# GpSimd adds at three borders, sums of squares in mid second gate and up, and ones by ones on TensorE at borders

## The reference, cut to what matters

```
# first stack
x = x + mix(rms_norm(x, g))
x = x + swiglu(rms_norm(x, g), w_gate_up, w_down)
# second stack
m = hybrid_rglru_mla(h) if layer % 2 == 0 else gated_delta_net(h)
x = x + rms_norm_2(m, norm_mix_post[layer])
h = rms_norm_2(x, norm_ffn_pre[layer])
x = x + rms_norm_2(swiglu_2(h, ...), norm_ffn_post[layer])
```

## Time and profile before

| | us |
|---|---|
| Runs shown: median (lowest, highest) of 3 | 2483.07 (2482.04, 2484.55) |
| The profiled execution: its own time | 2482.38 |
| The profiled execution: span of the page | 2480.6 |
| PE busy, DVE busy, ACT busy, POOL busy | 2309.6, 1563.7, 1186.7, 780.3 |

### The profile page before, as it was taken

How to read it: one execution, slowest core, us unless ns; L and a number is a source line. 1 busy time by engine, 2 the same in 40 slices (tenths; PEclk the granted TensorE clock), 3 DMA queues, 4 the chain that set the end, 5 groups by cost and what they waited for, 6 DMA issues and landing times.

```text
span 2480.6 us, 52063 instructions
## 1 busy us (share of the span) xinstructions
PE 2309.6 (93%) x20530; PEld 2218.5 (89%) x20530; DVE 1563.7 (63%) x2768; ACT 1186.7 (48%) x1956; POOL 780.3 (31%) x682
## 2 busy tenths in 40 slices
PE   7899787999999998899999999899997899999998
PEld 6899776999978988899999999789997898988997
DVE  3779787566631776666566666847667665536665
ACT  4544654544444665544444356544444445534333
POOL 1211588100068554300000037750003565554000
PEclk9999888999999999999999999999998999988999
DMA  4575200455536453455345554335552222223552
GB/s 172 202 200 179 95 1 1 136 195 183 173 125 193 142 140 114 137 186 177 128 162 183 181 164 147 123 99 188 184 186 75 74 78 88 76 86 118 181 192 85
DMA packets 103604, 344.30 MB, mean 139 GB/s; under 512 B 16400, under 2 KB 22064, under 8 KB 102912
## 3 DMA queue, kind: packets, MB, share of 16 engines
q1 hardware_dynamic: 102560, 339.61, 42.2%
q0 software_dynamic: 864, 2.16, 0.4%
HBM read 340.56 MB, written 1.16 MB: 138 GB/s over the span
## 4 chain that ended last, share of the span: by engine, by line
PE 69%; DVE 8%; ACT 4%; issue 2%; SPq 0%; POOL 0%; DMA 0%; DVEq 0%; ACTq 0%; POOLq 0%
PE ps L164 20%; PE ps L165 19%; PE ps L166 19%; ACT hi L102 1%; PE ps L289 1%; PE ps L1571 1%; DVE dr_aq L3338 1%; PE ps L3025 1%; DVE h_low L328 1%; PE ps L2976 1%; PE ps L1581 1%; DVE reciprocal_root L356 0%; PE ps L3018 0%; DVE lo L124 0%; PE ps L1594 0%
## 5 line engine op out<-in xcount | busy, mean ns | idle before, releaser
L164 PE MATMUL ps<-h_high,hi 128*128 128x256 f32 x3384 | 994.5, 294 | 47.1 <-DVE h_low L328 28.5
L165 PE MATMUL ps<-h_low,hi 128*128 128x256 f32 x3384 | 970.6, 287 | 0.0
L166 PE MATMUL ps<-h_high,lo 128*128 128x256 f32 x3384 | 970.2, 287 | 0.0
L102 ACT ACTIVATE hi<-raw 128x1024 fp32r<-128x1024 f32 x623 | 647.8, 1052 | 372.7 <-PE ps L166 371.8
L164 PEld LDWEIGHTS ps<-h_high,hi 128*128 128x128 f32 x3384 | 662.4, 196 | 65.6 <-DVE h_low L328 33.5
L165 PEld LDWEIGHTS ps<-h_low,hi 128*128 128x128 f32 x3384 | 663.2, 196 | 0.7
L166 PEld LDWEIGHTS ps<-h_high,lo 128*128 128x128 f32 x3384 | 662.3, 196 | 0.0
L124 DVE TENSOR_TENSOR lo<-raw,hi 128x1024 fp32r<-128x1024 f32 x422 | 509.7, 1224 | 214.4 <-ACT hi L102 213.9
L141 POOL TENSOR_TENSOR lo<-raw,hi 128x512 fp32r<-128x512 f32 x384 | 495.5, 1316 | 284.0 <-ACT hi L102 283.4
L164 PE MATMUL ps<-hidden_high,hi 128*128 128x256 f32 x1088 | 307.0, 282 | 5.0 <-DVE lo L124 3.3
L165 PE MATMUL ps<-hidden_low,hi 128*128 128x256 f32 x1088 | 308.6, 284 | 0.0
(11 more groups left out here) (470 smaller groups left out, 3278.2 us busy)
## 6 DMA issues: line engine op xcount, KB each, us to landing
raw<-in_weights SPq DMA_DIRECT2D x623, 512.0 KB, 3.5
at_bias<-bias_group SPq DMA_DIRECT2D x64, 64.0 KB, 2.8
consts<-in_consts SPq DMA_DIRECT2D x1, 1506.5 KB, 8.4
x<-in_x SPq DMA_DIRECT2D x1, 1024.0 KB, 4.8
s_cT<-in_s_b SPq DMA_DIRECT2D x1, 1024.0 KB, 7.5
s_cw<-in_s_c SPq DMA_DIRECT2D x1, 1024.0 KB, 9.5
s_parts<-in_s_bn SPq DMA_DIRECT2D x4, 256.0 KB, 9.3
s_cT<-s_rows POOLq DMA_DIRECT2D x16, 64.0 KB, 9.6
```

The costliest lines, as they stand in the source:

```text
L102: act.activation(k.hi[:, item % CUT, :], k.raw[:, item % RAW, :], ACT.Copy).then_inc(k.item_rounded, 1)
L164: pe.matmul(out, wh, xh, start=start, stop=False, **more)
L165: pe.matmul(out, wh, xl, start=False, stop=False, **more)
L166: return pe.matmul(out, wl, xh, start=False, stop=stop, **more)
```

## The change

Four things change, and one semaphore is shared to make room for a new one (`turned` replaces two).

- At the `POST` borders POOL does some of the adds of normed tiles to `x`: tiles 1 to 4 in the two feed-forwards, tiles 1 to 7 in the gated delta net. DVE keeps the others. POOL does them ahead of its adds of squares, or ahead of its weight cuts.
- In the two feed-forwards behind them, PE's sums of the new `x` move from before the second gate and up to its middle, between gate and up.
- PE multiplies ones by ones (128 x 128 by 128 x 128 in 32-bit floats, into PSUM bank 7) a number of times, ahead of the first gate and up: 20 at each of the three `POST` borders (after the sums of the result), 16 and 10 in the feed-forwards of layers 0 and 1, 8 in `glu`.
- The waits for `x` follow who writes the tile.

```diff
+def idle_products(k, pe, n):
+    for _ in range(n):
+        pe.matmul(k.ps[:, 7, 0:P], k.ones[:, :], k.ones[:, :], start=True, stop=True)
...
-    def __init__(self, k, gain_col, pending=0, post_col=None, cuts=True, adds=False):
+    def __init__(self, k, gain_col, pending=0, post_col=None, cuts=True, adds=False, idle=0):
+        self.idle = idle
+        self.pool_adds = () if pending != self.POST else range(1, KT - 3 if adds else KT)
+        self.b_px = k.x_added.n
+        k.x_added.n += len(self.pool_adds)
...
     def sums_before(self, pe):
         if self.pending == self.POST:
             self.sums(pe, 0)
+        idle_products(self.k, pe, self.idle)
...
     def gpsimd(self, pool):
-        for j in range(1, KT - 1):
+        for j in self.pool_adds:
+            pool.wait_ge(k.post_done.s, self.b_y + j + 1)
+            pool.tensor_tensor(k.x[:, j, :], k.x[:, j, :], k.post[:, j % 2, :], ALU.add).then_inc(k.x_added.s, 1)
+        for j in range(1, KT - 1) if self.adds else ():
...
     def vector(self, dve):
             if j < KT and self.pending == self.POST:
-                dve.wait_ge(k.post_done.s, self.b_y + j + 1)
-                dve.tensor_tensor(k.x[:, j, :], k.x[:, j, :], k.post[:, j % 2, :], ALU.add).then_inc(k.x_done.s, 1)
+                if j not in self.pool_adds:
+                    dve.wait_ge(k.post_done.s, self.b_y + j + 1)
+                    dve.tensor_tensor(k.x[:, j, :], k.x[:, j, :], k.post[:, j % 2, :], ALU.add).then_inc(k.x_done.s, 1)
...
             if j + 2 < KT and self.pending == self.POST:
-                dve.wait_ge(k.x_done.s, self.b_x + j + 1)
+                self.x_wait(dve, j)
                 normed(j + 2)
...
             def gate_up(i, b):
                 for half in range(2):
+                    if half == 1 and b == 1 and isinstance(i, int) and prep.pool_adds:
+                        prep.sums_after(pe)
...
             prep.x_read(pe)
-            prep.sums_after(pe)
+            if not prep.pool_adds:
+                prep.sums_after(pe)
...
 def glu(k, src, sg, pr, parts):
             w = Weights(k, pe, first)
+            idle_products(k, pe, 8)
...
-    swiglu(k, k.hp, Prep(k, VEC_AT["norm_ffn_pre_2"] + KT * layer, Prep.POST, VEC_AT["norm_mix_post_2"] + KT * layer, adds=True))
+    swiglu(k, k.hp, Prep(k, VEC_AT["norm_ffn_pre_2"] + KT * layer, Prep.POST, VEC_AT["norm_mix_post_2"] + KT * layer, adds=True, idle=20))
...
-    prep = Prep(k, VEC_AT["norm_mix_pre_2"] + KT, Prep.POST, VEC_AT["norm_ffn_post_2"], cuts=False)
+    prep = Prep(k, VEC_AT["norm_mix_pre_2"] + KT, Prep.POST, VEC_AT["norm_ffn_post_2"], cuts=False, idle=20)
...
+        prep.gpsimd(pool)
         late_cut(k, pool, late)
         cut(0, 8)
...
-    swiglu(k, k.hp, Prep(k, VEC_AT["norm_ffn_g"] + KT * layer, adds=True), side)
+    swiglu(k, k.hp, Prep(k, VEC_AT["norm_ffn_g"] + KT * layer, adds=True, idle=(16, 10, 0, 0)[layer]), side)
```

More of the change, by code:

```diff
@@ L252, in __init__ @@
         if pending:
-            k.x_done.n += KT
+            k.x_done.n += KT - len(self.pool_adds)
         if pending == self.POST:
@@ L272, in scalar @@
             if self.pending:
-                act.wait_ge(k.x_done.s, self.b_x + j + 1)
+                self.x_wait(act, j)
             else:
@@ L316, in here, with x_wait @@
         pe.wait_ge(self.k.low_done.s, self.b_l + j + 1)
+    def x_wait(self, engine, j):
+        if j in self.pool_adds:
+            engine.wait_ge(self.k.x_added.s, self.b_px + self.pool_adds.index(j) + 1)
+        else:
+            engine.wait_ge(self.k.x_done.s, self.b_x + sum(i not in self.pool_adds for i in range(j + 1)))
     def x_read(self, pe):
         if self.pending:
-            pe.wait_ge(self.k.x_done.s, self.b_x + KT)
+            pe.wait_ge(self.k.x_done.s, self.b_x + KT - len(self.pool_adds))
+            if self.pool_adds:
+                pe.wait_ge(self.k.x_added.s, self.b_px + len(self.pool_adds))
     def vector(self, dve):
@@ L820, in __init__ @@
         self.V, self.A, self.side, self.rows = k.s5v, k.s5a, k.side_here, k.s5_rows
-        self.flipped, self.masked = k.s5_flipped, k.s5_masked
+        self.flipped, self.masked = k.turned, k.s5_masked
         self.v, self.a0, self.s0 = k.s5v.n, k.s5a.n, k.side_here.n
@@ L927, in done @@
         self.k.s5a.n += 6
+        self.flipped.n += 1
         self.k.s5v.n = self.v
@@ L2724, in gdn_heads @@
     g.x = k.sem("gdn_x_updated")
-    g.xt = k.sem("gdn_x_turned")
     g.u = k.sem("gdn_u_in_psum")
@@ L2737, in gdn_heads @@
     V, A = k.s5v, k.s5a
+    g.xt, b_xt = k.turned.s, k.turned.n
     v0, a0, i0 = V.n, A.n, k.side_here.n
-    prep = Prep(k, VEC_AT["norm_mix_pre_2"] + KT, Prep.POST, VEC_AT["norm_ffn_post_2"], cuts=False)
+    prep = Prep(k, VEC_AT["norm_mix_pre_2"] + KT, Prep.POST, VEC_AT["norm_ffn_post_2"], cuts=False, idle=20)
     late = k.late
@@ L2966, in _ @@
                     pe.wait_ge(g.pc, 10 * hg + 2 * (l - 2) + a + 1)
-                    pe.wait_ge(g.xt, 10 * hg + 2 * (l - 2) + a + 1)
+                    pe.wait_ge(g.xt, b_xt + 10 * hg + 2 * (l - 2) + a + 1)
                     if l == LEVELS:
@@ L3363, in _ @@
                     if l == 1:
-                        dve.wait_ge(g.xt, 10 * hg + a + 1)
+                        dve.wait_ge(g.xt, b_xt + 10 * hg + a + 1)
                         dve.transpose(X[:, a, :, :], XT[:, a, :, :]).then_inc(g.x, 1)
@@ L3548, in build @@
         k.low_odd = counted("low_part_odd_tile")
+        k.x_added = counted("x_tile_updated_by_gpsimd")
         k.silu_done = counted("silu_done")
@@ L3564, in build @@
         k.s5_rows = counted("s5_lambda_rows")
-        k.s5_flipped = counted("s5_lambda_in_rows")
+        k.turned = counted("turned_over")
         k.s5_masked = counted("s5_drive_table")
```

## The result

| | median us | lowest to highest | executions |
|---|---|---|---|
| before | 2478.36 | 2473.63 to 2484.55 | 20 |
| changed | 2486.07 | 2481.75 to 2499.53 | 20 |

The ratio is 1.0032, with a 95% interval of 1.0023 to 1.0040: the change makes the kernel 7.9 us slower (5.7 to 9.9). The three executions shown ahead of the prediction lay high; twenty put the median of before at 2478.4. So the forecast of 2485.5 came within 0.6 of 2486.1 by luck: the starting time was 4.7 too high, and the difference (+2.5) was a third of the measured one. What went wrong is the difference, and the rest of this text is about it.

A forecast was written before the change was run, and what follows sets the result against it. PE, busy for 93% of the span, was taken as the bound. Terms +1.35 - 0.95 + 3.4 - 1.3 = +2.5 on 2482.38 gave 2484.9, or 2485.5 against the median; range 2480.5 to 2490.5.

The forecast's parts named there:

- no change: Whole kernel: the time stays within 0.2% of before, chance 0.64.
- Rival 3: Two feed-forward borders: idle stretch before first down costs the clock; one fall about 2488, both 2489 to 2492; chance 0.22.
- The moved sums: Second gate and up, two feed-forward borders: sums start 2.9 later, 7.03 to first down stays; price +1.7 each, +3.4.
- The collisions: POST borders: POOL adds and DVE two-input operations delay each other, 0.89 a pair; first gate and up still 1.2 sooner.
- Rival 4: POST borders: POOL's adds of x do not collide with DVE's low parts; time 2478; chance 0.08.
- The clock: Last border: twenty products of ones fill PE's wait for nothing, and the clock should stay at 2.4 GHz.
- Layer 0: Start of layer 0's feed-forward: 16 products of ones run past the barrier's opening; +1.35, ends -0.3 and +3.0.
- glu and layer 1: Ones at glu gain -0.95, other end 0; ones ahead of layer 1's feed-forward lie in a wait, 0.
- The passes of ones: PE's products of ones: two passes each, 0.11 a pass at full clock; the page gives 56 ns.
- Rivals 1 and 2: Layer 0: ones stream as fast as cut products, 2482.3, chance 0.05; or clock holds at the barrier, 2483.9, chance 0.17.
- Rival 5: Ones by ones don't hold the clock, so layer 0 runs at half clock (+7.1); 2493.5; chance 0.06.

## Why the prediction was right and wrong

**The time lay in the range, the sign of the difference was the forecast's, its size was not**: +2.5 forecast, "no change" at 0.64; measured +7.9, over the 0.2% for which I had 0.28. Rival 3 had this size: over the 2482.4 that it started from, its times are +5.6 for one fall and +6.6 to +9.6 for both. But only half of the falls behind the measured figure are its own.

**The moved sums: right.** "PE comes to them after 24 matmuls more, 2.9 later": measured 2.85 to 2.89, four times over. And "nothing in the 7.03 from the sums to the first down is shortened": 7.03 again. This is what the change does against its own aim, and it could be read from the chain view of before.

**The collisions: right in kind, sized a little too well.** DVE's and POOL's instructions in time, last border of the changed kernel, beside the earlier trace rows:

```profile
2265.53 0.88 DVE L355 SCALAR_TENSOR_TENSOR normed_result<-ps,vec,reciprocal_root 128x256 f32<-128x256 f32 x2
...
2267.31 1.03 DVE L351 SCALAR_TENSOR_TENSOR h_low<-x,vec,h_high 128x256 fp32r<-128x256 f32 x1
...
2268.66 0.47 DVE L351 SCALAR_TENSOR_TENSOR h_low<-x,vec,h_high 128x256 fp32r<-128x256 f32 x1
...
2269.45 0.56 DVE L351 SCALAR_TENSOR_TENSOR h_low<-x,vec,h_high 128x256 fp32r<-128x256 f32 x1
...
2273.44 0.95 DVE L351 SCALAR_TENSOR_TENSOR h_low<-x,vec,h_high 128x256 fp32r<-128x256 f32 x1
2274.31 0.95 DVE L368 TENSOR_TENSOR x<-x,normed_result 128x256 f32<-128x256 f32 x1
2275.18 1.34 DVE L351 SCALAR_TENSOR_TENSOR h_low<-x,vec,h_high 128x256 fp32r<-128x256 f32 x2
```
```profile
2266.48 1.57 POOL L322 TENSOR_TENSOR x<-x,normed_result 128x256 f32<-128x256 f32 x2 [5.87 <-DVE normed_result L355]
2268.81 1.79 POOL L322 TENSOR_TENSOR x<-x,normed_result 128x256 f32<-128x256 f32 x2 [0.76 <-DVE normed_result L355]
2270.56 5.29 POOL L327 TENSOR_TENSOR h<-h 128x256 f32<-128x256 f32 x6
```

Low parts 1 to 3 come every 0.8 to 0.9 and those of tiles 4 to 6 every 1.75, as worked out (0.89, 1.78), and the last one ends at 11.0 for 10.7. The first is the one I missed: POOL's second add, begun at the same moment, held it for 1.03, to 2.8 after the first normed where I had 2.3. So the gain is 0.8 a border and not 1.2. In the delta net it is the same: its first low part took 1.03 too, and it gave 0.9 against the one trace and not 1.3. That a DVE operation with two inputs in SBUF stands while a GpSimd one reads SBUF is what the Trainium skill, SBUF — State Buffer, section Who interferes with whom, states; the trace agrees (0.95 beside a GpSimd add, 0.47 alone). Rival 4, no collision, is excluded.

**The clock: the step that failed (the fall in the gate and up).** I wrote "The clock should stay at 2.4 GHz; I have used that above". It stayed through the wait, and fell later, when tiles came every 1.75 and PE was busy for 0.7 of each: 1.5 lost at both borders. I had the two facts, the slow tiles and the full clock, and did not set one beside the other. The extra ones at tiles 5 to 7 took that fall away, which shows it.

The other fall was rival 3, at 0.22. It happened in 9 of 10 cases, and was worth 1.5 in seven of them, just under the 1.7 of its lower end, and 2.5 in two. I gave it little weight since PE's clock had held in the wait of 3.35 ahead of layer 1. That one row was an exception: in the kernels that have the same wait there without ones, the clock fell in five of six executions. The idle stretch was 3.4 from matmul to matmul where I had 3.0, about as long as that wait.

**Layer 0: the path right, its price right only against one trace.** The barrier opened as I read it:

```profile
72.82 0.98 PE L234 MATMUL ps<-ones 128*128 128x128 f32 x3 [3.21 <-PEq L629]
```
```profile
79.07 0.36 PE L164 MATMUL ps<-h_high,hi 128*128 128x256 f32 x1
...
84.91 0.59 PE L313 MATMUL ps<-h,ones 128*128 128x256 f32 x2
```

The ones ran for 6.2, mostly at half clock. In this execution the stretch to the sums was 15.6 for 13.1 (+2.5, near my upper end), in the four others with ones 14.5 (+1.4, where I had +1.35). But the 13.1 of the trace that I read was itself high: without ones the median is 11.9. So the ones cost 2.6 up to the sums, and 1.2 up to the norm behind the feed-forward.

**glu and layer 1: the total right, the places by luck.** Against the trace of before it is -0.85 for -0.95 at glu and 0 for 0 at layer 1. In the five other executions without ones it is 0 at glu and -0.6 to -0.9 at layer 1. My term of 0 for layer 1 came from the one execution in six in which the clock held there.

**The passes of ones**: forty in 4.63 are 0.11 each, as in the earlier trace rows. The Trainium skill, TensorE: Matmul & The Clock Gate, section Back-to-back issue gap, gives 56 ns for 128 columns for a matmul by itself, and some 81 ns in a stream of weight loads and matmuls. The prediction used the first, where these passes are such a stream. An estimate by the page is 2.2 or 3.2 for the forty; the trace, with 4.63, agrees with neither for these 32-bit products. Rivals 1 and 2 fall with it and with the clock, which was at half from 71.6, before the first of the ones. Rival 5 falls too: ones by ones held the clock at all three borders.

With the measured terms the sum is: 2 x (2.87 - 0.8) = 4.1 for the borders; 2 x 1.14 = 2.3 for the gate and up (the mean of the six borders with adds, ones and moved sums, without the extra ones); 2 x 1.49 = 3.0 behind the first down; -0.8 for the delta net and -0.8 for glu with layer 1 (15.59 and 63.21 against medians of 16.4 and 64.0 without); +1.2 for layer 0. That is 9.0, inside 5.7 to 9.9.

## What to carry to other kernels

Before you move work on an engine that runs in order, take the distance from that work to whoever waits for its result, and see whether anything in it gets shorter; if not, the consumer is late by exactly what you put in front. A faster supply is worth only as much as the consumer can take at the clock it has, and a consumer that was slow and steady may become fast and gappy: look at how busy it will be in each stretch, and ask where its clock falls then. Filling a wait keeps the clock at its high level there. But if the fall only moves into a stretch of dense work, it costs what it did not cost in the wait. And one trace shows one course of the clock: a row in which it held is no rule, and a stretch in which it was half for long makes a change look better there than it is. Here three such stretches (layer 0, glu, layer 1) read otherwise in most of the other executions.

## What the runs showed that I had not expected

The granted clock fell while PE was working, after a stretch with 1.86 busy of 3.4, in 8 of 10 borders; I had looked for falls only in idle stretches. With less help (GpSimd's adds but no ones) the same border was faster, 21.0 against up to 22.6, because the half clock then lay in the wait and in the first tiles, where PE waits for DVE anyway.

Two executions of one kernel differ in stages that nothing was changed in: the S5 stage took 148.4 to 155.1 and the delta net behind its border 379 to 388, while a dense feed-forward without a fall repeated to 0.02 (183.03 to 183.05 in nine executions). What makes those two stages vary was not tried.
